# Constants' own semaphore, last stage's rows loaded in the last expert blocks with roots by three tiles, and mLSTM weights times scores directly behind log weights

## The reference, cut to what matters

```python
mod = silu(cond) @ w_ada + b_ada                      # shift, scale, gate of both sub-layers
hn = rmsnorm(x, norm1) * (1 + sc1) + sh1
q, k, v, o, gt, xr, gr = split(hn @ w_in)
# mLSTM, chunk by chunk, forward and backward, 4 heads x 128
s = einsum(q, k) * exp(log_d - m_t)                   # scores times weights
num = w_inter * (q @ C) + s @ v
den = w_inter * (q @ n) + sum(s)
h = num / maximum(abs(den), exp(-m_t))
C_new = decay * C + einsum(w_s, k, v)
# RG-LRU beside it, output projection, gated residual
x = x + g1 * mix
hn2 = rmsnorm(x, norm2) * (1 + sc2) + sh2
y = moe(hn2)                                          # 64 experts, 8 of them for each row, and a shared one
x = x + g2 * y
out = rmsnorm(x, norm_final)
```

## Time and profile before

| | |
|---|---|
| median of 3 runs | 2458.14 us (2456.18 to 2460.27) |
| profiled execution | 2452.43 us, span 2450.7 us |
| TensorE busy | 2045.1 us, 83% of the span |
| VectorE / ScalarE / GpSimd busy | 1286.7 / 1012.7 / 689.4 us |
| moved by DMA | 424.52 MB, 173 GB/s on the mean |

### The profile page before, as it was taken

How to read it: one execution, slowest core, us unless ns; L and a number is a source line. 1 busy time by engine, 2 the same in 40 slices (tenths; PEclk the granted TensorE clock), 3 DMA queues, 4 the chain that set the end, 5 groups by cost and what they waited for, 6 DMA issues and landing times. The chain is left out here.

```text
span 2450.7 us, 30697 instructions
## 1 busy us (share of the span) xinstructions
PE 2045.1 (83%) x8155; PEld 1336.8 (55%) x8156; DVE 1286.7 (53%) x2145; ACT 1012.7 (41%) x1458; POOL 689.4 (28%) x648
## 2 busy tenths in 40 slices
PE   2776998999868979817999999999999999999940
PEld 0232433447767835405766666676666666666730
DVE  1547343300456758855555555565555454555547
ACT  0334433200112311105665555666665555556631
POOL 4010010000000012452344444443444444444420
PEclk7898998999879989958999999999999999999975
DMA  9422230110100063109978989867888989996454
GB/s 264 132 81 85 69 104 18 43 35 18 27 1 1 6 252 117 69 28 340 320 205 282 318 249 323 231 172 198 247 278 273 351 268 317 299 301 176 106 149 180
DMA packets 114241, 424.52 MB, mean 173 GB/s; under 512 B 22933, under 2 KB 37269, under 8 KB 89229
## 3 DMA queue, kind: packets, MB, share of 16 engines
q1 hardware_dynamic: 62508, 261.05, 28.8%
q0 software_dynamic: 51376, 162.80, 26.4%
q10 hardware_dynamic: 304, 0.02, 0.0%
HBM read 338.68 MB, written 85.66 MB: 173 GB/s over the span
## 5 line engine op out<-in xcount | busy, mean ns | idle before, releaser
L1726 DVE TENSOR_TENSOR wupl<-w,wuph 128x2048 fp32r<-128x2048 f32 x232 | 521.4, 2289 | 546.4 <-ACT wuph L1692 546.4
L1692 ACT ACTIVATE wuph<-w 128x2048 fp32r x232 | 432.0, 1916 | 37.9 <-SPq L1522 34.0
L1643 PE MATMUL bank<-w,hT 128*128 x912 | 414.1, 597 | 0.7 <-issue 0.3
L1625 PE MATMUL bank<-wuph,xTh 128*128 128x512 f32 x920 | 370.1, 402 | 22.1 <-DVE xTl L1735 22.0
L1625 PE MATMUL bank<-wuph,xTl 128*128 128x512 f32 x920 | 361.9, 393 | 0.0
L1625 PE MATMUL bank<-wupl,xTh 128*128 128x512 f32 x920 | 361.0, 392 | 0.0
L1643 PEld LDWEIGHTS bank<-w,hT 128*128 128x128 f32 x912 | 165.0, 191 | 169.2 <-issue 169.1
L1577 POOL DMA_INDIRECT xg<-hn_scratch,idx_g x118 | 215.4, 1825 | 96.0 <-POOL idx_g L1569 93.9
L1585 POOL DMA_INDIRECT yacc_scratch<-y,idx_s x114 | 185.1, 1623 | 113.8 <-ACT y L1683 67.0
L1682 ACT ACTIVATE y<-bank 128x512 f32<-128x512 f32 x114 | 68.2, 598 | 358.1 <-POOLq L1582 201.9
L1625 PEld LDWEIGHTS bank<-wuph,xTh 128*128 128x128 f32 x920 | 174.6, 190 | 61.3 <-issue 27.5
(11 more groups left out here) (312 smaller groups left out, 2340.9 us busy)
## 6 DMA issues: line engine op xcount, KB each, us to landing
w<-in_exp_w SPq DMA_DIRECT2D x192, 1024.0 KB, 9.0
wada<-in_w_ada POOLq DMA_DIRECT2D x16, 1024.0 KB, 5.9
wg<-in_w_in SPq DMA_DIRECT2D x12, 1024.0 KB, 5.5
x<-x_scratch SPq DMA_DIRECT2D x18, 512.0 KB, 4.0
wada<-in_w_ada SPq DMA_DIRECT2D x4, 2048.0 KB, 21.2
yacc_scratch<-zero POOLq DMA_DIRECT2D x10, 512.0 KB, 9.1
x_scratch<-x SPq DMA_DIRECT2D x9, 512.0 KB, 2.6
hn_scratch<-hn SPq DMA_DIRECT2D x9, 512.0 KB, 2.9
```

The costliest lines, as they stand in the source:

```text
L1625: mm = pe.matmul(b_up[j][:, :], x[:, k, :], w[:, :, k, :], start=(k == 0 and i == 0), stop=(k == KT - 1 and i == 2))
L1643: mm = pe.matmul(b_down[half][:, :], hT[:, i, :], w2[:, bass.ds(slot, 1), i, half * 512:(half + 1) * 512].rearrange("p s n -> p (s n)"), s ...
L1692: act.activation(part13(wup[j][0], half), raw13(e % WSLOT, half), ACT.Copy).then_inc(w_high, 1)
L1726: dve.tensor_tensor(part13(wup[j][1], half), raw13(e % WSLOT, half), part13(wup[j][0], half).bitcast(F32), ALU.subtract).then_inc(w_low, 1)
```

## The change

Four edits.

1. The first of the small loads, the constants, counts on a semaphore of its own, `s_cst`; the first `spread` waits for that alone, and TensorE waits for the other nineteen ahead of the first gate matmul.
2. The gate matmul of tiles 1 to 4 stands behind tile 8 in `seq` and no longer behind tile 5.
3. In `stage_mlstm` the product of exponentials and scores stands directly behind the log weights of the same unit, ahead of the wait for the products of the unit before.
4. SyncE loads all nine tiles of `x`, the gate rows and the norm's row into the space of `w13`, at the end of the expert stage, as soon as the last split of weights has been made. In the last stage `y` has nine buffers, and roots are taken for three tiles at a time.

```diff
@@ -201,7 +201,7 @@
...
         s_x1, s_posc = sem("st_x1"), sem("ld_posc")
-        s_cc, bd_zero = sem("ld_cc"), sem("bd_zeroed")
+        s_cc, s_cst, bd_zero = sem("ld_cc"), sem("ld_consts"), sem("bd_zeroed")
...
@@ -212,14 +212,14 @@
         w_in = a["w_in"][0].rearrange("(k p) n -> p k n", p=P)
         NG = FIRST_MODS
         small = small_loads(a, m)
-        m.ld_all = 16 * len(small)
+        m.ld_all = 16 * (len(small) - 1)
 
         TAKE = {0: [0, 1], 1: [2, 3], 2: [4, 5], 3: [6, 7, 8]}
         seq = [("mod", g) for g in range(NG)]
         for t in range(NT):
             seq.append(("turn", t))
             for g, (t0, nt) in enumerate(SPANS):
-                if t == min((t0 + nt) // P, NT - 1):
+                if t == (1 if g == 0 else NT - 1):
                     seq.append(("gate", g))
         jobs_before, n = {}, 0
         for item in seq:
@@ -260,7 +260,7 @@
                     r = 2 * (t - 1)
                     pool.dma_start(posr[t % PS], a["pos_row"][r:r + 2, :].unsqueeze(1).to_broadcast([2, 64, 512])).then_inc(s_x[t], 16)
                 for dst, src in small[3 * t:3 * t + 3]:
-                    pool.dma_start(dst, src, allow_slow_non_contiguous=True).then_inc(m.ld, 16)
+                    pool.dma_start(dst, src, allow_slow_non_contiguous=True).then_inc(s_cst if dst is small[0][0] else m.ld, 16)
                 if t == 0:
                     pool.memset(m.bd[:, :, :, :, :], 0.0).then_inc(bd_zero, 1)
             pool.wait_ge(x_hn, 1)
@@ -276,7 +276,7 @@
             def spread(g):
 
                 if g == 0:
-                    pe.wait_ge(m.ld, m.ld_all)
+                    pe.wait_ge(s_cst, 16)
                 pe.wait_ge(mod_row, g + 1)
                 for s in range(2):
                     j = 2 * g + s
@@ -306,6 +306,8 @@
                         ring.filled(mm)
                 else:
                     t0, nt = SPANS[t]
+                    if t == 0:
+                        pe.wait_ge(m.ld, m.ld_all)
                     bank = ring.fill()
                     pe.wait_ge(free, jobs_before["turn", (t0 + nt) // P - 1] + 2)
                     for k in range(KT):
@@ -1080,6 +1082,9 @@
                         ins = dve.scalar_tensor_tensor(eb[(n + 1) % 2][:, h, :], PM[:, h * P:(h + 1) * P],
                                                        m.cols[:, j, 0, h:h + 1], m.neg[d], ALU.add, ALU.add)
                     ins.then_inc(logw, 1)
+                    dve.wait_ge(weights, n + 2)
+                    e = eb[(n + 1) % 2]
+                    dve.tensor_tensor(e[:, :, :], e[:, :, :], PS[:, :].rearrange("p (h t) -> p h t", h=H), ALU.mult).then_inc(probs, 1)
                 if 0 <= n < U:
                     d, c, second = units[n]
                     seq, j = min(c, 1), d * NT + c
@@ -1095,10 +1100,6 @@
                         ins = dve.scalar_tensor_tensor(st, st, m.decb[:, h, d, c:c + 1], px(8 + h), ALU.mult, ALU.add)
                     ins.then_inc(unit_done, 1)
                     dve.wait_ge(unit_done, n + 1)
-                if n + 1 < U:
-                    dve.wait_ge(weights, n + 2)
-                    e = eb[(n + 1) % 2]
-                    dve.tensor_tensor(e[:, :, :], e[:, :, :], PS[:, :].rearrange("p (h t) -> p h t", h=H), ALU.mult).then_inc(probs, 1)
                 if 0 <= n < U:
                     dn = nd[:, :, P]
                     link(dve.scalar_tensor_tensor(d1[:, :], dn, -1.0, dn, ALU.mult, ALU.max))
@@ -1431,7 +1432,7 @@
     with ExitStack() as ctx:
...
-        w13 = sb("w13", [P, WSLOT, 2, KT, DE])
+        w13 = m.w13
...
 
@@ -1555,6 +1556,12 @@
             issue_down(NE)
             for e in range(NE - 1, NX):
                 down_landed(e, e // WSLOT + 1)
+            sp.wait_ge(w_low, pairs(sp) * 4 + 4)
+            for t in range(NT):
+                sp.dma_start(m.late[:, t, :], m.x2[t * P:(t + 1) * P, :]).then_inc(m.s_late, 16)
+            for s in range(2):
+                sp.dma_start(m.late[:, NT + s, :], m.mods[s:s + 1, 5 * D:6 * D].to_broadcast([P, D])).then_inc(m.s_late, 16)
+            sp.dma_start(m.late[:, NT + 2, :], a["norm_final"].unsqueeze(0).to_broadcast([P, D])).then_inc(m.s_late, 16)
 
         @block.gpsimd
         def _(pool):
@@ -1755,34 +1762,28 @@
     with ExitStack() as ctx:
...
-        x, y = [sb(f"x6_{j}", [P, D]) for j in range(3)], [sb(f"y6_{j}", [P, D]) for j in range(3)]
...
-        s_in, s_x, s_out = sem("ld_final"), [sem(f"ld_x6_{j}") for j in range(3)], [sem(f"st_y{j}") for j in range(3)]
+        BATCH = 3
+        x = [m.late[:, t, :] for t in range(NT)]
+        gate, nfrow = [m.late[:, NT + s, :] for s in range(2)], m.late[:, NT + 2, :]
+        y, sq = [sb(f"y6_{t}", [P, D]) for t in range(NT)], sb("sq6", [P, D])
+        ss, rs, rt = sb("ss6", [P, NT]), sb("rs6", [P, NT]), sb("rt6", [P, NT])
+        ri = sb("ri6", [P, NT], I32)
+        s_y, s_out = [sem(f"ld_y6_{t}") for t in range(NT)], sem("st_y")
...
 
         @block.sync
         def _(sp):
-            for s in range(2):
-                sp.dma_start(gate[s][:, :], m.mods[s:s + 1, 5 * D:6 * D].to_broadcast([P, D])).then_inc(s_in, 16)
-            sp.dma_start(nfrow[:, :], a["norm_final"].unsqueeze(0).to_broadcast([P, D])).then_inc(s_in, 16)
             for t in range(NT):
-                if t >= 3:
-                    sp.wait_ge(s_out[t % 3], 16 * (t // 3))
-                sp.dma_start(x[t % 3][:, :], m.x2[t * P:(t + 1) * P, :]).then_inc(s_x[t % 3], 16)
-                sp.dma_start(y[t % 3][:, :], m.yacc[t * P:(t + 1) * P, :]).then_inc(s_x[t % 3], 16)
+                sp.dma_start(y[t][:, :], m.yacc[t * P:(t + 1) * P, :]).then_inc(s_y[t], 16)
 
         @block.gpsimd
         def _(pool):
             for t in range(NT):
                 pool.wait_ge(y_new, t + 1)
                 dst = o[0][0] if t == 0 else o[1][0, (t - 1) * P:t * P, :]
-                pool.dma_start(dst, x[t % 3][:, :]).then_inc(s_out[t % 3], 16)
-            for j in range(3):
-                pool.wait_ge(s_out[j], 16 * ((NT + 2 - j) // 3))
+                pool.dma_start(dst, x[t]).then_inc(s_out, 16)
+            pool.wait_ge(s_out, 16 * NT)
 
...
         def _(act):
@@ -1790,28 +1791,35 @@
                 act.wait_ge(x_new, t + 1)
                 if t >= 1:
                     act.wait_ge(x_sq, t)
-                act.activation(sq[:, :], x[t % 3][:, :], ACT.Square, accum_out=ss[:, t:t + 1]).then_inc(x_sq, 1)
+                act.activation(sq[:, :], x[t], ACT.Square, accum_out=ss[:, t:t + 1]).then_inc(x_sq, 1)
 
         @block.vector
         def _(dve):
             link = Chain(dve, dch)
 
             def add(t):
-                dve.wait_ge(s_x[t % 3], 32 * (t // 3 + 1))
-                yt, xt = y[t % 3][:, :], x[t % 3][:, :]
-                link(dve.tensor_tensor(yt, yt, gate[min(t, 1)][:, :], ALU.mult))
-                dve.tensor_tensor(xt, xt, yt, ALU.add).then_inc(x_new, 1)
-
-            dve.wait_ge(s_in, 48)
-            add(0)
-            for t in range(NT):
-                if t + 1 < NT:
-                    add(t + 1)
-                dve.wait_ge(x_sq, t + 1)
-                v = ss[:, t:t + 1]
+                dve.wait_ge(s_y[t], 16)
+                link(dve.tensor_tensor(y[t][:, :], y[t][:, :], gate[min(t, 1)], ALU.mult))
+                dve.tensor_tensor(x[t], x[t], y[t][:, :], ALU.add).then_inc(x_new, 1)
+
+            def root(t0):
+                c = slice(t0, t0 + BATCH)
+                dve.wait_ge(x_sq, t0 + BATCH)
+                v = ss[:, c]
                 link(dve.tensor_scalar(v, v, 1.0 / D, EPS, ALU.mult, ALU.add))
-                newton_rsqrt(link, dve, v, rs[:, :], rt[:, :], ri[:, :])
-                dve.scalar_tensor_tensor(x[t % 3][:, :], x[t % 3][:, :], rs[:, :], nfrow[:, :], ALU.mult, ALU.mult).then_inc(y_new, 1)
+                newton_rsqrt(link, dve, v, rs[:, c], rt[:, c], ri[:, c])
+
+            dve.wait_ge(m.s_late, 16 * (NT + 3))
+            for t in range(BATCH):
+                add(t)
+            for t0 in range(0, NT, BATCH):
+                if t0 + BATCH < NT:
+                    add(t0 + BATCH)
+                root(t0)
+                for t in range(t0, t0 + BATCH):
+                    dve.scalar_tensor_tensor(x[t], x[t], rs[:, t:t + 1], nfrow, ALU.mult, ALU.mult).then_inc(y_new, 1)
+                    if t > t0 and t + BATCH < NT:
+                        add(t + BATCH)
 
 
 INPUTS = ["x_prompt", "x_sample", "c", "state_mlstm_C", "state_mlstm_n", "state_mlstm_m", "state_rglru_h", "c_ctx",
@@ -1876,6 +1884,9 @@
                 rows = [w[:, :, :].rearrange("p k n -> p (k n)")[:, j * D:(j + 1) * D] for w in m.wg for j in range(2)]
                 m.gate, m.shift, m.scale = rows[0:2], rows[2:4], rows[4:6]
                 stage_route(nc, a, m)
+        m.w13 = sb("w13", [P, WSLOT, 2, KT, DE])
+        m.late = m.w13[:, :, :, :, :].rearrange("p s w k n -> p (s w k n)").rearrange("p (t n) -> p t n", n=D)
+        m.s_late = sem("ld_late")
```

4 lines of the change are left out of this document (removed).

## The result

| | before | changed |
|---|---|---|
| median | 2457.56 us (2456.18 to 2460.27, 4 runs) | 2391.32 us (2389.16 to 2393.62, 4 runs) |
| ratio, 95% interval | | 0.9727 (0.9715 to 0.9739) |
| profiled execution | 2452.43 us, span 2450.7 | 2389.16 us, span 2387.4 |

The first stage, TensorE's timeline and then VectorE's. They answer to the earlier trace rows.

A forecast was written before the change was run, and what follows sets the result against it. TensorE, busy 83%, bounds the expert blocks, left alone; gains come from three other places. -12.0 + 1.8 - 33.5 - 21.0 = -64.7 us, against the 2458.1 median 2393 us, range 2380 to 2412.

The forecast's parts named there:

- the three places: Where TensorE is not the busy engine: first 135 us, mLSTM units around 640 to 870 us, last 85 us.
- Rival (f): Expert stage, 1236 us, gets a lower granted clock and the kernel is slower; 200 us low gives 2493; chance 0.02.
- (e): Nothing gained, because removed stalls are followed by others of the same length: 2458 us; chance 0.02.
- Part 1, the root: First stage: with the constants' own semaphore the nine-column root starts about 76.8 in place of 88.78, -12.0 us.
- Rival (d): First stage is held by its loads and half of the 12 us is gained: 2399 us; chance 0.07.
- Part 1, the gate matmul: First-stage tail: moved behind tile 8, first norm to end of gates takes 37.4 us, before 35.6; +1.8 us.
- Part 2, short units: mLSTM units 2 to 9: seven steps of 7.2 us in place of 11.94, VectorE's ring, -33.2 us.
- Rival (b): Clock stays low in the short mLSTM units, TensorE their bound at 8.6 us: 9.8 less gained, 2403; chance 0.10.
- Part 2, other steps: mLSTM: unit 9 to 10 gains 0.8 us, six long steps +0.4, unit 1 to 2 +0.7, last step -0.6.
- Part 3, roots and adds: Last stage on VectorE: three roots on three columns each, 44.1 us in place of 65.6.
- Part 3, the start: VectorE's last-stage start unchanged, 0: y 5.3 us earlier, scatters 5.3 later beside early rows; bounds -5.3 and +8.
- Rival (c): Early rows hold up both last scatters by the most the rows show: 8 us less gained, 2401; chance 0.09.

The follow-up runs named there:

- e3: Changed kernel with the gate matmul of tiles 1 to 4 back behind tile 5: 2391.39 us, ratio 0.974.
- e1: Kernel before with only the product moved directly behind the log weights: 2421.65 us, ratio 0.9859.
- e11: Kernel before with fifteen extra small matmuls filling TensorE's wait in the short units: 2457.38 us, ratio 1.0.
- e8: Changed kernel with the product behind the state update again for the long units, 1 and 10 to 17: 2392.92 us, ratio 0.974.
- e10: Changed kernel with eight of the twelve early rows loaded into free weight slots during the shared expert's blocks: 2386.21 us, ratio 0.9703.
- e6: Changed kernel with last-stage roots for one tile at a time: 2408.08 us, ratio 0.981.
- e12: Changed kernel with eight rows in free weight slots, long units' product behind the state update, gate matmul behind tile 5: 2385.93 us, ratio 0.9712.
- e2: Kernel before with only the constants' own semaphore: 2446.19 us, ratio 0.9959.
- e5: Kernel before with eight extra small matmuls filling part of TensorE's wait in the short units: 2452.87 us, ratio 0.9997.
- e7: Changed kernel without early loads, the twelve rows loaded in the last stage: 2389.59 us, ratio 0.9739.
- e4: Kernel before with only the last stage's edits (early rows, nine y buffers, roots by three tiles): 2434.7 us, ratio 0.9914.
- e9: Changed kernel with at most three loads of y in flight in the last stage: 2389.44 us, ratio 0.9738.

## Why the prediction was right

**The sum.** -63.3 us against -64.7 in the profiled executions. The median stands 2.2 us above the profiled one here (2391.32 to 2389.16) and not 5.7 as before. So the profiled execution fell 1.4 us short of the forecast gain and the median's distance was 3.6 less than assumed; that the two partly cancel is luck.

**What bounds the kernel.** Right: the three places were independent within what the intervals tell, and the expert stage kept its length (+0.2 us). The limit of 3 us that the prediction set for that stage is no firm sign, though: it is 1491.10 in e3, 1498.17 in e1 and 1499.30 in e11, which don't touch it. Rival (f), slower through that stage, didn't happen, nor did (e).

**Part 1, the root.** Forecast 76.8, measured 77.40, 76.83 to 79.04 over the kernels that have the edit. The chain named (last position row, two adds, square) is what the rows show. Rival (d) is out: the second add of that row ends at 76.08 (75.39 + 0.69), where 75.5 was the forecast.

**Part 1, the gate matmul.** Forecast 37.4 us from the first norm to the end of the gates, measured 38.40 in the changed kernel and up to 41.05 in others. The step that fell short is "the ninth tile is ready 9 x 2.47 = 22.2 us after the first norm starts": it left out that the gate matmul of tile 0 can run at the low clock and hold up the transposes. In the changed kernel that wait is the 1.13 us at 94.63, about the size of the miss (1.0); in e8 and e10 it is 1.97 and 1.87, and the clock falls once more ahead of the last matmuls. "TensorE is the bound of this tail, and 7 us of work that lay in its gaps lies at the end" is right in direction; between kernels with the same gate matmul of tile 0 the place costs 2.5 to 3.6 us and not 1.8.

**Part 2, short units.** Forecast 7.2 a step, measured 7.17 in steady state, 7.32 over the seven; the stall of 0.69 is 0.70 and the loop is VectorE's. -33.2 against -32.3. TensorE's share was taken nearly right: 5.2 us, where it is busy for 5.62 of 7.17, so the ring has 1.55 us of room below VectorE's. Rival (b), the low clock with TensorE as the bound, occurred in two steps of the seven (clock 0.68 and 0.77, 7.79 and 7.55 us) and cost 1.0 us together, not 9.8. That the denser loop would bring nearly the full clock was a choice and came true, 0.92 over the seven, but the fillers show that my reason for it, less idle time, isn't sufficient; to that extent it was luck.

**Part 2, other steps.** Unit 1 to 2 +0.86 (+0.7), 9 to 10 -0.95 (-0.8; in e3, e6, e8, e10 and e12 nothing, 12.20), six long steps +0.82 (+0.4), the last -0.59 (-0.6). By e8 the stall costs 2.5 us over the six steps; the +0.82 is that less the 1.7 us of one step at a low clock before.

**Part 3, roots and adds.** Forecast 44.1, measured 43.26. The roots are 16.8 of the 22.4 gained, by e6.

**Part 3, the start.** "Start unchanged, 0" measured -0.9 between unit 17 and the first add. The mechanism, `y` earlier and scatters later, is right, and over all profiles this distance is 1519.2 to 1521.8 us in five kernels without early rows (before, e1, e2, e5, e7; a sixth, e11, stands apart with 1527.2) and 1519.3 to 1522.3 in the six with them (changed, e3, e4, e6, e8, e9), but 1515.4 and 1510.7 in e10 and e12. The terms are another matter. With both scatters behind the split (e3, e6, e9) `y` comes 6.5 to 7.0 us earlier, where 5.3 was forecast, and the two delays are 7.1 to 8.5, where 5.3 was taken. In the changed kernel's profile `y` comes only 1.7 earlier and only the last scatter is late, by 4.0, and the scatter before it was issued 4.6 earlier against the split; there the near zero is in part luck. The sign named beforehand, the first add 17 to 18 us behind the last scatter's issue, failed: it was 19.88, and 13.8 to 14.2 in e3, e6 and e9. Rival (c), 8 us less gained, did not occur.

## What to carry to other kernels

When a ring of two engines waits on both sides, look for one instruction that holds a buffer for no reason but its place in the queue: moving it took 4.6 us off each of seven steps, though it put a new stall of 0.7 into them. A load that is issued early, but beside an operation that the end of the program waits for, only moves the wait; look for the stretch before it in which DMA has nothing urgent, which here made the difference between 0 and 5 us. Batch tiny dependent instructions over tiles: a root over three tiles costs what the root of one tile costs. And compare profiles only where the clock stood alike at the same place: here one matmul at the low level looked like 1.9 us of an edit.

## What the runs showed of the hardware

The granted clock of TensorE does not follow its busy share in the profile: 0.76 at 97% busy (81.33 of 83.90 us, a third of it fillers that contract over 4 rows) and 0.92 at 85% busy (43.56 of 51.20). A scatter with accumulation is held up by plain loads of another engine's queue in flight: the last two landed in 6.1 and 6.0 us before, and in 10.5 and 9.0 beside 6.3 MB of loads (e6; 9.9 and 9.2 in e9). And a load at the head of a queue was not held up by those issued behind it: with 16 loads issued by the time of the first add it was 10.4 us from the first issue to the add that needs five of them, with nine 10.3.
